# Last two layers: decayed keys and queries kept in place on VectorE, the recurrence's queries behind the attention's, the compression inside the attention's steps

## What is computed

```
# recurrence with decays, 4 heads of 128, chunks
f = lb + (1 - lb) * sigmoid(f_logit); k = 1 - f; qf = silu(q)
b = cumsum(log f)
A[t, s] = sum_d qf[t, d] * k[s, d] * exp(b[t, d] - b[s, d])   for s <= t
o = A @ v                      # then rms_norm(o) * silu(g)
# sparse attention, 8 query heads, 2 key heads of 64, three branches
kc, vc = compress(k_cmp), compress(v_cmp)      # silu(flat @ w1) @ w2 over windows of 32 tokens
o_cmp = softmax(q kc) vc
o_slc = softmax over selected blocks           # at 256 tokens all blocks
o_swa = softmax over a window of 512           # at 256 tokens all, causal
o = gate0 * o_cmp + gate1 * o_slc + gate2 * o_swa
x = x + concat(o_recurrence, o_attention) @ w_out
```

## Time and profile before

| | |
|---|---|
| median of three runs | 1440.23 us (1439.65 to 1442.6) |
| the profiled execution: time, span | 1444.79 us, 1443.0 us |
| instructions | 18641 |
| TensorE matmuls busy | 1359.7 us (94%) |
| VectorE busy | 880.3 us (61%) |
| ScalarE busy | 714.2 us (49%) |
| GpSimd busy | 192.4 us (13%) |
| mean granted TensorE clock | 0.970 of full |

### The profile page before, as it was taken

How to read it: one execution, slowest core, us unless ns; L and a number is a source line. 1 busy time by engine, 2 the same in 40 slices (tenths; PEclk the granted TensorE clock), 3 DMA queues, 4 the chain that set the end, 5 groups by cost and what they waited for, 6 DMA issues and landing times.

```text
span 1443.0 us, 18641 instructions
## 1 busy us (share of the span) xinstructions
PE 1359.7 (94%) x7251; PEld 1152.2 (80%) x7251; DVE 880.3 (61%) x1136; ACT 714.2 (49%) x1167; POOL 192.4 (13%) x206
## 2 busy tenths in 40 slices
PE   7879999999988999999989899999999898999998
PEld 5657888878777888888977778888888776788887
DVE  4875665665534656557764556666577555566665
ACT  6464554454454545446443345555464444455553
POOL 2211000011530300002322010000023220100000
PEclk9989999998999999999979999999999799999999
DMA  9333655544522555545431135555454311355551
GB/s 364 136 117 117 233 174 207 188 152 158 177 72 71 178 203 178 202 159 195 160 118 59 59 117 204 190 176 183 155 194 158 117 59 44 131 190 179 199 194 56
DMA packets 62328, 224.44 MB, mean 156 GB/s; under 512 B 7192, under 2 KB 7328, under 8 KB 62240
## 3 DMA queue, kind: packets, MB, share of 16 engines
q1 hardware_dynamic: 59616, 214.23, 42.7%
q0 software_dynamic: 1904, 6.82, 1.5%
q10 hardware_dynamic: 720, 2.19, 0.4%
HBM read 222.16 MB, written 1.05 MB: 155 GB/s over the span
## 4 chain that ended last, share of the span: by engine, by line
PE 81%; DVE 10%; ACT 5%; issue 3%; POOL 2%; DMA 0%; POOLq 0%; DVEq 0%; ACTq 0%
PE ps L277 15%; PE ps L281 15%; PE ps L282 15%; PE ps L323 15%; PE ps L327 7%; PE ps L423 3%; PE ps L458 2%; PE ps L330 2%; PE ps L481 2%; DVE wlo L1516 2%; PE ps L751 1%; ACT scr L993 1%; PE ps L329 1%; DVE xn L1555 1%; DVE small L1601 1%
## 5 line engine op out<-in xcount | busy, mean ns | idle before, releaser
L1516 DVE TENSOR_TENSOR wlo<-raw,whi 128x1024 fp32r<-128x1024 f32 (+1 forms) x402 | 485.7, 1229 | 295.3 <-ACT whi L939 293.7
L939 ACT ACTIVATE whi<-raw 128x1024 fp32r<-128x1024 f32 (+1 forms) x409 | 424.3, 1048 | 332.9 <-PE ps L323 178.6
L323 PE MATMUL ps<-XT,whi 128*128 128x512 f32 x896 | 318.6, 399 | 0.0
L327 PE MATMUL ps<-XT,wlo 128*128 128x256 f32 x896 | 251.7, 281 | 0.0
L323 PEld LDWEIGHTS ps<-XT,whi 128*128 128x128 f32 x896 | 168.5, 188 | 41.0
L277 PE MATMUL ps<-whi,HT_hi 128*128 128x512 f32 (+1 forms) x496 | 189.9, 383 | 6.8 <-DVE wlo L1516 6.3
L282 PE MATMUL ps<-whi,HT_lo 128*128 128x512 f32 (+1 forms) x496 | 188.4, 380 | 0.0
L281 PE MATMUL ps<-wlo,HT_hi 128*128 128x512 f32 (+1 forms) x496 | 188.0, 379 | 0.0
L327 PEld LDWEIGHTS ps<-XT,wlo 128*128 128x128 f32 x896 | 169.4, 189 | 1.2
L277 PE MATMUL ps<-whi,XT 128*128 128x512 f32 (+2 forms) x352 | 143.1, 407 | 16.7 <-DVE wlo L1516 7.9
L281 PE MATMUL ps<-wlo,XT 128*128 128x512 f32 (+2 forms) x352 | 137.8, 391 | 0.0
(11 more groups left out here) (253 smaller groups left out, 1933.6 us busy)
## 6 DMA issues: line engine op xcount, KB each, us to landing
raw<-in_w_m SPq DMA_DIRECT2D x152, 512.0 KB, 4.2
raw<-in_w_n SPq DMA_DIRECT2D x108, 512.0 KB, 4.2
raw<-in_w_c SPq DMA_DIRECT2D x48, 512.0 KB, 4.0
raw<-in_w_o SPq DMA_DIRECT2D x32, 512.0 KB, 3.5
raw<-in_w_kv SPq DMA_DIRECT2D x16, 512.0 KB, 4.1
raw<-in_w_b SPq DMA_DIRECT2D x16, 512.0 KB, 3.2
raw<-in_w_w SPq DMA_DIRECT2D x16, 512.0 KB, 4.2
raw<-in_w_a SPq DMA_DIRECT2D x12, 512.0 KB, 8.2
```

The source lines that it names most:

```text
L323: m = pe.matmul(outs[f][:, :], hi[:, j, at], both, start=(k == 0), stop=False)
L327: pe.matmul(outs[f][:, 0:T], lo[:, j, at], XT[0][:, k, :], start=False, stop=False)
L939: act.activation(whi[:, g % NSPLIT, 0:w], raw[:, g % NRAW, 0:w], ACT.Copy).then_inc(split_hi, 1)
L1516: dve.tensor_tensor(wlo[:, g % NSPLIT, 0:w], raw[:, g % NRAW, 0:w], whi[:, g % NSPLIT, 0:w].bitcast(F32), ALU.subtract).then_inc(split_lo, 1)
```

## The change

1. Levels. GpSimd's loop is gone. VectorE keeps the decayed keys (`KS`) and queries (`QF`) and multiplies them in place by one factor per block, broadcast over the block; it also multiplies the block decays pairwise (`decay_of`, 512 elements, then half each time, up to level 7). `advance(l)` waits for level l-1 on TensorE, as before, and for no other engine.
2. Order. `nq` comes before `hq` on TensorE, and the turned rows follow between and behind the last units of `hq`. The tanh of the recurrence's queries on ScalarE and `queries` on VectorE come behind those of the attention. GpSimd's rstd of the attention's queries has nothing else ahead.
3. Steps. All levels and all eight window units lie inside `attend`; levels 1 to 4 at `(1, 1)` to `(4, 1)`, level 5 at the start of step 5, 6 at `(5, 2)`, 7 at `(6, 2)`, 8 at `(7, 1)`. `weave` has a third piece in steps 1, 3 and 5. `hi` uses banks 0 and 3. `ch_turned` goes from `(2, 2)` to `(3, 2)`, `cmp_keys_values` from `(3, 2)` to `(4, 2)`, `hgrn_out` from steps 6 and 7 to step 8, `cmp_probs` and `cmp_out` about half a step later. VectorE's and ScalarE's dictionaries follow.

```diff
@@ TensorE
-                    yield from by_tile([f"hi{L}.0", f"hi{L}.1"], (0, 1), [a[w][16 + u] for u in range(4)], tok(XT))
+                    yield from by_tile([f"hi{L}.0", f"hi{L}.1"], (0, 3), [a[w][16 + u] for u in range(4)], tok(XT))
...
-                    if s < 2:
+                    if s < 2 or n in (0, 1, 3, 5):
                         next(tiles_left, None)
...
-                feature_pairs(f"hq{L}", (0, 1), [a[w][4 + u] for u in range(4)], {2: lambda: rows_turned((2,))})
-                block_of(f"nq{L}", w, 3, tok(XT), [2, 3], {1: lambda: level(0, 0), 2: lambda: level(0, 1), 3: lambda: level(1)})
-
+                block_of(f"nq{L}", w, 3, tok(XT), [2, 3], {2: lambda: rows_turned((2,))})
+                feature_pairs(f"hq{L}", (0, 1), [a[w][4 + u] for u in range(4)],
+                              {2: lambda: rows_turned((0,)), 3: lambda: rows_turned((1,))})
                 pe.wait_ge(ev("xclo"), i + 1)
-                next(tiles_left)
-                next(tiles_left)
-                level(2)
-                next(tiles_left)
-                next(tiles_left)
-                rows_turned((0, 1))
...
-                    {(0, 1): lambda: level(3),
-                     (1, 1): lambda: level(4),
-                     (2, 1): lambda: level(5), (2, 2): ch_turned,
-                     (3, 1): lambda: level(6), (3, 2): cmp_keys_values,
-                     (4, 1): lambda: level(7),
-                     (5, 1): lambda: level(8),
-                     (6, 2): lambda: (cmp_keys_turned(), hgrn_out(0)),
-                     7: lambda: cmp_scores(0), (7, 1): lambda: cmp_scores(1), (7, 2): lambda: hgrn_out(1),
-                     (9, 2): cmp_probs,
-                     (10, 1): lambda: cmp_out(0), (10, 2): lambda: cmp_out(1),
+                    {(0, 1): lambda: level(0, 0), (0, 2): lambda: level(0, 1),
+                     (1, 1): lambda: level(1), (2, 1): lambda: level(2), (3, 1): lambda: level(3), (4, 1): lambda: level(4),
+                     5: lambda: level(5), (5, 2): lambda: level(6), (6, 2): lambda: (level(7), cmp_keys_turned()),
+                     (7, 1): lambda: (level(8), cmp_scores(0)), (7, 2): lambda: cmp_scores(1),
+                     (3, 2): ch_turned, (4, 2): cmp_keys_values,
+                     8: lambda: hgrn_out(0), (8, 2): lambda: hgrn_out(1),
+                     10: cmp_probs, (10, 2): lambda: cmp_out(0), 11: lambda: cmp_out(1),
                      12: hgrn_rows}, (6, 6), weave)
@@ ScalarE
-                queries_in()
...
-                hidden_in(0)
                 turned_in((0, 1))
+                queries_in()
...
-                     {2: lambda: hidden_in(1), 3: ch_in, 4: cmp_in, 6: values_in,
+                     {2: lambda: hidden_in(0), 3: lambda: hidden_in(1), 4: ch_in, 5: cmp_in, 6: values_in,
@@ GpSimd
-                for l in range(1, LEVELS):
...
-                    chain(pool, "p_chain", pool.tensor_tensor(Sv[:, :, 0, :], Sv[:, :, 0, :], bc(tot, 2, m_), ALU.mult))
-                    pool.tensor_tensor(Fv[:, :, 1, :], Fv[:, :, 1, :], bc(lastf, 2, m_), ALU.mult).then_inc(ev("lev"), 1)
@@ VectorE
                     if l <= LEVELS:
-                        m_ = 1 << (l - 1)
+                        m_ = 1 << (l - 2)
                         v = lambda t: t.rearrange("p (n two m) -> p n two m", two=2, m=m_)
-                        dve.wait_ge(ev("lev"), 8 * i + l)
-                        dve.tensor_tensor(v(X)[:, :, 0, :], v(K)[:, :, 0, :], v(S)[:, :, 0, :], ALU.mult)
-                        dve.tensor_tensor(v(X)[:, :, 1, :], v(Q)[:, :, 1, :], v(F)[:, :, 1, :], ALU.mult).then_inc(ev("xlev"), 1)
-                    if l > 1:
-                        take(l - 1)
+                        G = decay_of[l - 1].rearrange("p (n two) -> p n two", two=2)
+                        if l > 2:
+                            dve.wait_ge(ev("decay_of"), (LEVELS - 2) * i + l - 2)
+                        dve.tensor_tensor(v(KS)[:, :, 0, :], v(KS)[:, :, 0, :], bc(G[:, :, 1], 2, m_), ALU.mult)
+                        dve.tensor_tensor(v(QF)[:, :, 1, :], v(QF)[:, :, 1, :], bc(G[:, :, 0], 2, m_),
+                                          ALU.mult).then_inc(ev("xlev"), 1)
+                    take(l - 1)
+                    if l < LEVELS:
+                        dve.tensor_tensor(decay_of[l], G[:, :, 0], G[:, :, 1], ALU.mult).then_inc(ev("decay_of"), 1)
...
-                soft(tags, {0: lambda: advance(3), 1: lambda: advance(4),
-                            2: lambda: (advance(5), ch_silu(1)),
-                            3: lambda: (branch(1, 0), advance(6), cmp_values()),
-                            4: lambda: (advance(7), key_sums(), cmp_values_in()),
-                            5: lambda: advance(8), 6: lambda: advance(9),
-                            7: lambda: branch(1, 1),
-                            8: lambda: (cmp_scores(), hgrn_sums(0)),
-                            9: lambda: (branch(2, 0), cmp_probs(), hgrn_sums(1)),
-                            10: gates,
+                soft(tags, {0: lambda: (advance(1), diagonal(0)), 1: lambda: (diagonal(1), advance(2)),
+                            2: lambda: (advance(3), ch_silu(0)),
+                            3: lambda: (branch(1, 0), advance(4), ch_silu(1)),
+                            4: lambda: (advance(5), cmp_values()),
+                            5: lambda: (advance(6), key_sums(), cmp_values_in()),
+                            6: lambda: advance(7),
+                            7: lambda: (branch(1, 1), advance(8)),
+                            8: lambda: (cmp_scores(), advance(9)),
+                            9: lambda: (branch(2, 0), cmp_probs(), hgrn_sums(0)),
+                            10: lambda: (hgrn_sums(1), gates()),
                             11: lambda: (hgrn_rows(), cmp_add(0), cmp_add(1))})
```

More of the change, by code:

```diff
@@ L734, in level @@
                             c = h * T + half * P
-                            m = pe.matmul(out[:, h * P:(h + 1) * P], kk[:, c:c + P], q[:, c:c + P], start=True, stop=True)
+                            m = pe.matmul(out[:, h * P:(h + 1) * P], KS[:, c:c + P], q[:, c:c + P], start=True, stop=True)
                         close(f"{name}.{half}", m)
@@ L741, in level @@
                         for h in range(4):
-                            m = pe.matmul(out[:, h * P:(h + 1) * P], X[:, h * T:h * T + P],
-                                          X[:, h * T + P:(h + 1) * T], start=True, stop=True)
+                            m = pe.matmul(out[:, h * P:(h + 1) * P], KS[:, h * T:h * T + P],
+                                          QF[:, h * T + P:(h + 1) * T], start=True, stop=True)
                         close(name, m)
@@ L749, in level @@
                             c = h * T + tt * P
-                            q2 = X[:, c:c + P].rearrange("p (n two m) -> p n two m", two=2, m=s)[:, :, 1, :]
-                            m = pe.matmul(out[:, (tt * 4 + h) * 64:(tt * 4 + h + 1) * 64], X[:, c:c + P], q2,
+                            q2 = QF[:, c:c + P].rearrange("p (n two m) -> p n two m", two=2, m=s)[:, :, 1, :]
+                            m = pe.matmul(out[:, (tt * 4 + h) * 64:(tt * 4 + h + 1) * 64], KS[:, c:c + P], q2,
                                           start=True, stop=True)
@@ L855, in rows_turned @@
                                       for ty in range(2) for h in range(2)])
-                            turn(f"zT{L}.{tt}.{g}", (6, 3)[tt], tiles)
+                            turn(f"zT{L}.{tt}.{g}", 6 + tt, tiles)
                 block_by_token(f"A{L}", w, 2, tok(XT), [0, 1], after_norm(k), True)
@@ L1448, in _ @@
                 norm(6 + 2 * i)
-                F, S = slot(0, 1024), slot(7, 1024)
                 f = fills[f"n{6 + 2 * i}.1.1"]
@@ L1871, in _ @@
                     step(dve.tensor_tensor(A4, A4, B4, ALU.add))
-                F, K, S, Q, X = slot(0, 1024), slot(1, 1024), slot(7, 1024), slot(8, 1024), slot(9, 1024)
+                F, KS, S, Q, QF = slot(0, 1024), slot(1, 1024), slot(7, 1024), slot(8, 1024), slot(9, 1024)
+                decay_of = {1: F}
+                for l in range(2, LEVELS):
+                    decay_of[l] = S[:, 1024 - (2048 >> (l - 1)):1024 - (1024 >> (l - 1))]
                 n30 = 2 * NCMP
@@ L1940, in decays @@
                     step(m)
-                    dve.tensor_scalar(K, F, -0.5, 0.5, ALU.mult, ALU.add).then_inc(ev("hfk"), 1)
+                    step(dve.tensor_scalar(KS, F, -0.5, 0.5, ALU.mult, ALU.add))
                 def queries():
@@ L1973, in advance @@
                 def advance(l):
-                    if l > 1:
-                        f = fills[f"lev{L}.{l - 1}"]
-                        splits(f.pos + AHEAD)
-                        dve.wait_ge(bank_full[f.bank], f.turn)
+                    if l == 1:
+                        dve.tensor_tensor(QF, Q, F, ALU.mult).then_inc(ev("xlev"), 1)
+                        return
+                    f = fills[f"lev{L}.{l - 1}"]
```

(16 more changed lines are left out.)

26 lines of the change are left out of this document (10 added, 16 removed).

## The result

The changed kernel took **1472.18 us** (median of 4 runs, 1465.62 to 1474.53), the kernel before 1440.53 beside it (4 runs, 1439.65 to 1442.6): ratio 1.0212, 95% interval 1.0182 to 1.0241, or 31 us slower. The forecast was 1453 with a range of 1434 to 1463. The sign is right; the loss is about two and a half times the one forecast, and the time is outside the range.

What follows compares the result with a forecast made beforehand. TensorE bounds the stage, lengthened by waits and half clock behind them. Per layer 25.8 us go and 33.2 come, +7.4; with a second count's +5.6, 6.5 taken, twice +13: 1457.8 profiled, 1453 on the runs' scale, range 1434 to 1463.

Steps and rivals of the forecast that it cites:

- the "issue" wait at `hi`: First weave of hi: TensorE's 3.4 us wait for bank 1, freed in ch_silu(1), goes with banks 0 and 3.
- the cover of 3.4: Taken back per layer because half clock lengthens TensorE's cover: 1.6 at the low half, 1.8 before (4,2).
- The arithmetic at nothing: Levels moved from GpSimd to VectorE: worth 0, since no TensorE wait names GpSimd's multiplies.
- the upper bound of 0.4 a level: VectorE's in-place level multiplies: at most a third dearer, from a 1.64 us broadcast multiply against a 1.22 add.
- the clock term: Half clock behind new waits at (1,1), (3,2), (4,2) and the tail: 3.15 us each, 12.6 a layer.
- The second count of the prediction: Steps laid end to end at full clock to the output projection: 830.3 instead of 833.9, -3.6; with the clock +5.6.
- The middle between two counts: Per-layer net taken between +7.4 (sum of waits and clock) and +5.6 (steps end to end): 6.5, twice +13.
- the first count: Per-layer sum of waits and clock in stage and tail: 25.8 us gone, 33.2 new, net +7.4.
- Longer echoes: Rival: clock stays down between (3,2) and (4,2) and once more in the tail; +4 a layer, 1461; chance 0.14.
- The clock holds: Rival: same waits in the stage, but TensorE isn't dropped to half clock behind them; 1435, faster; chance 0.16.
- VectorE is early: Rival: VectorE is at its level when it closes; (1,1) and low-half waits go, (3,2) falls to 3.5; 1437; chance 0.12.
- an even trade: Rival: waits in the stage change places and the time stays the same, 1440; chance 0.08.

Runs made afterwards that it cites:

- the repeat: The changed kernel run again without any edit, for a second profile: 1473.47 us, ratio 1.0195 to the kernel before.
- The filled waits: The changed kernel with products of zeros put in TensorE's waits before level 1, both compression products and the second cmp_out: 1449.23 us, ratio 1.0052.
- the kernel with all edits: The changed kernel with compression one step later, diagonal(1) in step 0, advance(9) before cmp_scores and second cmp_out in bank 1: 1428.79 us, ratio 0.9887.

## Why the prediction was right in sign and wrong in size

**Which waits go and come.** Right, all of them, at their lines. Forecast and measured: `ch_turned` 6.0 and 5.8; `cmp_keys_values` 4.7 and 4.1; second `cmp_out` 3.9 and 3.7; `level(1)` 2.5 and 2.3; `cmp_probs` 2.7 and 1.6; low half 1.6 and 0.5; banks 0 and 7 2.4 and 1.8 (1.0 and 0.8); the first turned queries 0.2 more and none; the wait for the queries between `nq` and attention and the "issue" wait at `hi` gone. The new terms 17.4 + 6.6 = 24.0 less the cover of 3.4 make 20.6; the stage shows 21.9, of which 2.2 are waits that both kernels have (L458 and the first of the output projection), so 19.7. The waits that go, 13.2 in the sum, are 13.2 in the trace. Adding the durations of a chain over three engines from the view's rows held for the longest one: 5.4 + 2.5 for `ch_turned` came out as 7.9. For the low half and `cmp_probs` it was 1.1 too high.

**The arithmetic at nothing.** Right within what the runs can tell: 1.0014 alone, with an interval to 1.0044. The in-place multiplies take 0.69 us (746.32 above) as the old ones did, so the upper bound of 0.4 a level from the earlier trace rows did not apply. The 1.64 us that it rested on was not the price of a broadcast operand: the same multiply takes 1.22 us in the changed kernel, where GpSimd's level multiplies are gone.

**The step that failed: the clock term, "four, at 3.15 each, 12.6", less the 3.4 taken back.** The new stage's clock was put at 9.2 us a layer. The second count of the prediction lets this be measured: it laid the steps end to end at full clock and came to 154.5 us for the stage (830.3 less the start at 675.8). The stage took 169.8 and 172.0, which leaves 15.3 and 17.5 for the clock if that count of the steps is right: 6.1 and 8.3 more than the sum had, 14.4 in both. In the repeat it leaves 15.7 and 21.2, 1.6 of the latter a longer wait for a low half. By windows the layer-2 stage loses 20.8 (part of it falls into waits) against 13.8 of before.

The places were right where waits were long, but the new stage was given the old one's clock, four echoes at the old mean. The filled waits gave back 12.1 a layer, where the term had 9.2: that is 2.9 of the 6.1 and 8.3. The rest, 3.2 and 5.4, fits the stretch of 0.74 from 800 us, which loses 5.2. It has no wait over 1.3 ahead, is there in both layers of both profiles (0.74 and 0.74, 0.74 and 0.75), stayed in layer 2 when the waits were filled (0.75), and stood in no list, so the sum had it at nothing. Why the clock falls there these runs do not show. The last two figures are differences of differences; that the echoes were priced too low and a stretch without a wait was left out is what the windows and the filled waits show.

**The middle between two counts.** The two counts differ by 1.8 in the net of the waits, and the forecast took the middle, 6.5 a layer, which compares with 11.7 and 14.2 measured. The trace's own net of the waits is 6.4 and 7.4. So the first count's 7.4, whose clock terms cancel, has the waits right, and the change of clock that it put at nothing is what is missing.

**The scale.** The two stages grew by 25.9 us in the first trace, and 1440.2 and 25.9 are 1466. The last 6 us of 1472 come from where the half clock fell in the executions profiled. The forecast took 4.6 off because the profile of before lay so far above its median. The trace of after lay 6.6 below its own: 0.97 in 300 to 460 us, where before and the repeat of the changed kernel have 0.94, and 0.88 in 1080 to 1260 us, where the repeat has 0.86. The repeat's span of 1470.0 is close to the median, and its two stages grew by 30.0. So the 6 are a draw of the profiled execution, as far as two profiles can tell.

**The rivals.** "Longer echoes" (0.14) is what came, in kind: the clock down longer around (4,2) and once more late in the stage. Its place was off (between (3,2) and (4,2) the clock was up again) and its price, 4 a layer above the forecast, too small by 2 to 4. "The clock holds" and "VectorE is early" are refuted by the windows and by the 2.8 us that VectorE was late, "an even trade" by the time. The lateness came, as said, from high halves that ScalarE issues behind exponentials, and no GpSimd work was involved: that engine is idle from 702 to 768 us. That the sign came out right owes nothing to luck in the waits, but it hangs on the two compression products alone: one step later the same change is at 0.9951.

## What to carry to other kernels

When engines hand a step round (level, maximum, exponentials, copy, next product), lay the chain out from the timeline's starts, and ask of each product moved into the step which copy of the *same* step it needs: two products placed one step too early cost 9.9 us a layer in waits and made the change lose; one step later it came to 0.9951. Price a wait on TensorE at its length plus a clock term of its own, up to the longest stretch seen and not the mean, and widen the range by it: here two waits of 9.9 us a layer came with some 8 us of clock. To learn what the clock behind waits is worth, fill the waits with products of zeros, in the waits and not among other products: what comes back is not dependence.

## What the runs showed that was not expected

- A window of 0.74 (780 to 800 us) came in one execution and of 1.00 in another of the same program, with the same 19.25 us of busy TensorE and the same waits. What decides it these runs do not show. The Trainium skill (TensorE: Matmul & The Clock Gate, "What's actually happening") says of the slow phase at the start of a kernel that it is "run-variable"; these two windows agree with that for one in the middle. The Trainium skill (TensorE: Matmul & The Clock Gate, "HAM oscillation — how this bites in real kernels") tells of the slow phase in the middle of a kernel behind waits for transfers. Here much of it came behind waits for ScalarE and VectorE of 2.3 to 5.8 us, and some behind none.
- A 512-column product, 0.22 to 0.24 us from start to start among its like, cost 0.49 between products of 15 columns.
- The masked copy of 512 elements took 1.31 us at the two lowest levels and 0.70 above them. I had read the longer one as contention with GpSimd. In the kernel with all edits, where GpSimd is idle, it is there still; what differs between the levels is the length of the blocks that the mask takes, one and two elements at the lowest two. No run varied that alone. Timeline, VectorE of that kernel:

```profile
727.07 1.32 DVE L1946 COPY_PREDICATED scr<-const,ps 128x512 f32<-128x512 uint32 x1
...
749.64 0.70 DVE L1946 COPY_PREDICATED scr<-const,ps 128x512 f32<-128x512 uint32 x1
```

- Contention with GpSimd is seen all the same, in other instructions. In layer 2 of the kernel before, beside GpSimd's level multiplies, the rope multiply took 1.64 us and two low halves 1.80 and 1.75; in the changed kernel and in the one with the levels on VectorE the multiply takes 1.22 and 1.21, and the low halves of the stage 1.22 in the mean (1.28 before). The Trainium skill (SBUF — State Buffer, "Who interferes with whom") has VectorE and GpSimd share a read port that a VectorE instruction with two SBUF inputs needs, and these durations agree with it. In time it was worth nothing that can be told (1.0014). Timeline, VectorE before, then the same multiply after:

```profile
717.84 1.64 DVE L2119 TENSOR_TENSOR scr<-scr,mixf 128x1024 f32<-128x1024 f32 x1
...
696.98 1.22 DVE L2101 TENSOR_TENSOR scr<-scr,mixf 128x1024 f32<-128x1024 f32 x1
```
